# The last rotations and the bias's mask, moved ahead of the value turns and the last key chunk

## The reference

```python
h = modulate(x, sh1, sc1)
u = h @ w_in_l
q_a = apply_axial_rope(split_heads(u[..., OFF_AQ:OFF_AK], A_Q_HEADS), *rope)
k_a = apply_axial_rope(split_heads(u[..., OFF_AK:OFF_AV], A_KV_HEADS), *rope)
v_a = split_heads(u[..., OFF_AV:OFF_BQ], A_KV_HEADS)
q_b, k_b, v_b = ...                     # slices of u too, 4 heads each
o_a = window_gqa_latent(q_a, k_a, v_a, kc_a, vc_a, a_sink[l])
o_b = neighbourhood_latent(q_b, k_b, v_b, kc_b, vc_b, nat_bias[l])
o_c = conformer_conv(u[..., OFF_C:], conv_w[l], conv_b[l], conv_ln_g[l], conv_ln_b[l])
o = jnp.concatenate([o_a, o_b, o_c], axis=-1) @ w_out[l]
```

## Time and profile before

| | |
|---|---|
| median of 3 executions | 2954.65 us (2952.22 to 2955.24) |
| the profiled execution | 2943.12 us |
| its span, first to last instruction | 2941.3 us, 35988 instructions |
| mean granted TensorE clock | 0.961 of full speed |
| PE busy | 2727.4 us, 93% of the span |
| VectorE, ScalarE busy | 991.0 us, 622.2 us |
| DMA | 582 MB, mean 198 GB/s |
| `project2` up to its end, first layer | barrier seen by PE at 1229.4 us |
| `project2` up to its end, second layer | barrier seen by PE at 2252.3 us |

### The profile page before, as it was taken

How to read it: one execution, slowest core, us unless ns; L and a number is a source line. 1 busy time by engine, 2 the same in 40 slices (tenths; PEclk the granted TensorE clock), 3 DMA queues, 4 the chain that set the end, 5 groups by cost and what they waited for, 6 DMA issues and landing times. The chain is left out here.

```text
span 2941.3 us, 35988 instructions
## 1 busy us (share of the span) xinstructions
PE 2727.4 (93%) x15314; PEld 1573.6 (53%) x15314; DVE 991.0 (34%) x2175; ACT 622.2 (21%) x1297; POOL 63.4 (2%) x61
## 2 busy tenths in 40 slices
PE   8998879899999989899679999999798986999998
PEld 7776645588874456574333333333585743444443
DVE  3513445223330238385611111111573752111212
ACT  4222215211110111272401000000313621000102
POOL 0000000000000000000001111111000000000000
PEclk9999979999999999999889999999898998999999
DMA  4137671122222031100369999999120027999995
GB/s 156 65 116 284 231 312 37 72 72 79 79 86 88 0 141 44 43 2 29 143 248 371 385 384 387 381 390 392 52 72 29 16 104 295 404 422 422 422 422 238
DMA packets 87476, 582.00 MB, mean 198 GB/s; under 512 B 10186, under 2 KB 11754, under 8 KB 21780
## 3 DMA queue, kind: packets, MB, share of 16 engines
q1 hardware_dynamic: 78244, 554.66, 47.9%
q0 software_dynamic: 6544, 21.24, 2.5%
q10 hardware_dynamic: 2528, 3.80, 0.3%
HBM read 561.96 MB, written 17.70 MB: 197 GB/s over the span
## 5 line engine op out<-in xcount | busy, mean ns | idle before, releaser
L1998 PE MATMUL ps<-both,ring 128*128 128x257 f32 x1408 | 308.6, 381 | 1.6 <-PEq L1628 1.6
L2911 PE MATMUL ps<-ring,xsL 128*64 128x512 f32 x1320 | 297.5, 602 | 5.7 <-ACTq L217 5.7
L1998 PEld LDWEIGHTS ps<-both,ring 128*128 128x128 f32 x1408 | 268.2, 191 | 42.0 <-issue 1.9
L2911 PEld LDWEIGHTS ps<-ring,xsL 128*64 128x64 f32 x1320 | 100.7, 139 | 193.7 <-issue 187.7
L3142 DVE TENSOR_TENSOR hidL<-hidL,ps 128x1024 f32<-128x1024 f32 x16 | 19.5, 1222 | 463.7 <-PE ps L2911 463.7
L1816 PE MATMUL ps<-ring,actT 128*128 128x512 f32 x352 | 153.6, 598 | 6.9 <-PEq L1986 6.9
L2510 PE MATMUL ps<-both,ring 128*128 128x384 f32 x480 | 157.5, 490 | 1.9 <-PEq L1809 1.9
L2911 PE MATMUL ps<-ring,htL 128*64 128x512 f32 x640 | 145.2, 605 | 3.4 <-ACTq L217 3.2
L856 PE MATMUL ps<-both,ring 128*128 128x264 f32 x640 | 143.8, 386 | 1.5 <-PEq L633 1.5
L3172 ACT ACTIVATE hidL<-ps 128x1024 f32<-128x1024 f32 x16 | 16.4, 1024 | 555.2 <-PE ps L2919 318.5
L856 PEld LDWEIGHTS ps<-both,ring 128*128 128x128 f32 x640 | 121.4, 190 | 23.0 <-issue 2.4
(11 more groups left out here) (536 smaller groups left out, 3671.6 us busy)
## 6 DMA issues: line engine op xcount, KB each, us to landing
ring<-in_w_exp SPq DMA_DIRECT2D x245, 1024.0 KB, 12.9
ring<-in_w SPq DMA_DIRECT2D x73, 1024.0 KB, 5.1
tokens_b<-in_w_exp SPq DMA_DIRECT2D x63, 1024.0 KB, 12.4
ring<-in_w_mod SPq DMA_DIRECT2D x48, 1024.0 KB, 5.2
h<-in_w_exp SPq DMA_DIRECT2D x37, 1024.0 KB, 17.1
lent<-in_w_exp SPq DMA_DIRECT2D x26, 1024.0 KB, 15.5
both<-in_w_exp SPq DMA_DIRECT2D x13, 1024.0 KB, 18.1
gb<-in_rows SPq DMA_DIRECT2D x8, 512.0 KB
```

The source lines that it names most:

```text
L1998: mm = pe.matmul(k.ps[:, 4 * (j % 2) + 2 * gv + h, 0:HALF], w(c_), hT[:, c_, FIRST + h * HALF:FIRST + (h + 1) * HALF], start=c_ == 0, stop ...
L2911: mm = pe.matmul(ps[HD * par:HD * par + HD, bank + half, :], lhsL(kk, par), weights(kk)[:, half, par, :], start=kk == 0, stop=kk == KD - 1 ...
```

## The change

The change alters the order of statements only; no instruction is added or removed. On PE, `rotate(3)` moves from behind job 19 to behind `turn_back`, which follows job 17. `rotate(4)` moves from behind job 20, the last one, to behind job 18. `turn_values` stays behind job 19. On VectorE the mask's six passes move ahead of the three copies to `vb`.

```diff
                 elif i == VB:
                     turn_back()
+                    rotate(3)
+                elif i == VB + 1:
+                    rotate(4)
                 elif i == KB:
-                    rotate(3)
                     turn_values()
-                elif i == KB + 1:
-                    rotate(4)
...
             for r in range(2, 5):
                 rope(r)
-            dve.wait_ge(turned.sem, turned.of(1))
-            for t in range(0, NT2, 2):
-                at = 4 * BANK + t * 2 * P
-                steps.free(dve.tensor_copy(vb[:, t:t + 2, :], psf[:, at:at + 4 * P].rearrange("p (t c) -> p t c", t=2)))
             dve.wait_ge(z_done.sem, z_done.of(1))
             to, mt = 0, 0
             for _, lo, hi in NEAR_PIECES:
...
                 steps.free(dve.tensor_tensor(out, mask, src, ALU.subtract))
                 to, mt = to + GRID_H * w, mt + w
+            dve.wait_ge(turned.sem, turned.of(1))
+            for t in range(0, NT2, 2):
+                at = 4 * BANK + t * 2 * P
+                steps.free(dve.tensor_copy(vb[:, t:t + 2, :], psf[:, at:at + 4 * P].rearrange("p (t c) -> p t c", t=2)))
             steps.join()
```

## The result

The changed kernel took 2935.44 us (median of 4, 2932.73 to 2936.02) against 2954.94 us for the kernel before: a ratio of 0.9943, 95% interval 0.9929 to 0.9957, so 12.7 to 21 us less. (The two medians are 19.5 us apart, which would be a ratio of 0.9934; the ratio of 0.9943 stands for 16.8 us.) The prediction was 13.5 us less. Over all timed executions of the two, 15 of the changed kernel average 2936.2 us and 59 of the one before 2951.4, a difference of 15 us. The four of the kernel before in the first comparison average 2954.4 us: its 19.5 us caught that kernel at the upper end of its scatter.

What follows compares the result with a forecast made beforehand. The prediction took PE's wait for VectorE at the barrier ending `project2` as the bound. 11.8 us from that wait plus 1.7 from the clock made 13.5 less: 2954.65 to 2941.1 us, 8-in-10 range 2935 to 2946.5.

Steps and rivals of the forecast that it cites:

- What bounds: Barrier ending `project2`: VectorE alone, late behind PE's last rotation, makes PE wait 7.57 us per layer.
- The rotations and the mask: In `project2`: moved rotations add no PE wait; mask and copies run beside jobs 18 to 20, at no cost.
- The wait that is left: Barrier ending `project2`: ScalarE becomes last, PE idles about 1.65 us; 5.9 us less per layer, 11.8 in all.
- Passed on: Behind attention: the experts' weight stream moves forward with PE, costed at nothing; rival of gain not passed on, chance 0.07.
- My sign of being wrong: Wrong if the second layer's experts end less than 9 us earlier; other signs were a long wait or late SP or ScalarE.
- The clock: Start of attention: first score group at full clock, then a fall; 0.87 us per layer, 1.7 in all, bounds 0 to 6.3.
- holds in one layer: Rival, chance 0.27 for one or both layers: clock stays full in attention; one layer gives about 2.2 us more.
- a later fall lands worse: Part of the rival of no clock gain or a little loss elsewhere, chance 0.15: 9 to 12 us less in all.
- my reading of it on the barrier's idle time alone: Attention: idleness cut from 7.57 to about 1.65 us would leave 2.4 GHz in both layers, the upper case, 18 us.
- The sum: Whole kernel: 11.8 us from the barrier wait plus 1.7 from the clock, 13.5 us less, 2941.1 us.
- the range: Whole kernel's time, 8 in 10: 2935 to 2946.5 us.

Runs made afterwards that it cites:

- a late VectorE: Changed kernel with the mask's six passes done eight times over on VectorE; ratio 1.0010 to the kernel before.
- The filled runs: Constant matmuls added: 16 or 8 behind the last rotation of the kernel before (1.0051, 0.9996), or in the changed kernel's gaps (0.9944; with split copies 0.9949).
- the two with filled gaps: Changed kernel with constant matmuls behind job 20 and the first two score groups, ratio 0.9944 to before; the same with the last key product's copies split, 0.9949.
- the one with both edits: Changed kernel with constant matmuls in PE's gaps and the last key product copied by ScalarE and VectorE; ratio 0.9949 to before, median 2936.1 us.

## Why the prediction was right

**What bounds.** Right: the last rotation, issued last, made VectorE late, and no other engine was. Rotation 4 alone gives the full gain, rotation 3 and the mask none, and a late VectorE takes it all back.

**The rotations and the mask.** Costed at nothing, no wait added: right. The rotations wait for nobody; the mask ended at 1211.29, 18.8 us behind the start of `turn_back`, where I had computed 18.7. The cover of the copies is the last job, about 10 us: they end 9.63 us before ScalarE does; my times gave 1223.04 - 1213.4 = 9.6.

**The wait that is left.** Forecast 5.9 us per layer, measured 6.03 by the wait and 6.01 and 5.90 by the stages. The barrier behind ScalarE took 0.31 us where I had put 0.45 (0.39 by the earlier trace rows), so the wait that is left, 1.54 us, is just under the 1.6 that I had called the shortest. The 5.90 us of the second layer are less than the wait's 6.03 because PE's own part of that stage took 0.12 us more.

**Passed on.** Right: the final norm starts as much earlier as the stages before it say, and the experts' DMA stream moves along with PE. The two stages that the change does not touch differ by +0.87 and +0.08 us. In the first of them PE was at half clock for about 3 us more (77.9 us against 74.7), so what I had costed at nothing took 0.95 us in this profile; in the two further ones it took 0.90 us and gave 1.3. My sign of being wrong, experts that end less than 9 us earlier, was badly put: in this profile the final norm starts only 7.4 us earlier, because the first 1046 us took 6.2 us longer; counted from the first `project2` it is 13.6.

**The clock.** This term was mis-sized, within its bounds. Forecast 0.87 us in each layer, 1.7 in all; measured 1.90 + 0.73 = 2.6. The mechanism that I took for likeliest, first group at full clock and a fall behind it, is what the second layer does. In the first layer the clock held through all of attention, so that VectorE took the first head's result 11.6 us after the start of attention instead of 14.7, and 1.3 of these 3.2 us went again in a fall in the gate rows, a place where the kernel before had none in this layer. The two further profiles of the changed kernel show the same. My "holds in one layer" and "a later fall lands worse" thus both happened, in one profile. The filled runs show that the gaps between the score groups matter: the clock fell with 0.71 and with 0.30 us of idleness at the barrier, and it held in both layers once the gaps were filled. In the second layer it fell in all five profiles with a wait of 1.54 or 1.26 us and open gaps, and held in the two with filled gaps. But in the first layer it held through the same open gaps in four of those five, and fell there in the two with less idleness at the barrier, 0.71 and 0.30 us. What decides between these is open. The rule of the Trainium skill ("TensorE: Matmul & The Clock Gate", Part 1), that activity holds the clock and its lack brings it down, agrees with the filled runs; my reading of it on the barrier's idle time alone, full clock in both layers, does not: after 1.54 us the clock fell in the second layer. Why the same open gaps did no harm in the first layer, the rule as I read it doesn't say.

**The sum.** 11.8 + 1.7 = 13.5 forecast; 11.9 + 2.6 = 14.5 in the stages; 15 on average over the executions. The first median of 19.5 us less lies at the edge of the range (2935.4 against 2935.0). I had read the scatter of the kernel before off three executions, 2952 to 2955 us; fifty-nine of them range from 2944.9 to 2956.4. In the stages that it was made of, the forecast was 1 us short, not 6. That the whole stretch to the final norm gives 13.6 us, almost the forecast, is in part luck: the clock gave 0.9 us more than I took, and the untouched stages took 0.95 us that I had left out; in one of the further profiles the same stretch gives 15.4 us.

## What to carry to other kernels

At a block's end look at what hangs on the last instruction of the busiest engine: here a matmul of 0.86 us that another engine had to follow with 7 us of passes cost TensorE 6 us per layer, and one job earlier it cost nothing. Moving it as far as just ahead of one long job was enough; the order of the passes behind it did not matter. And judge such an edit by the stages it touches: in three profiles of the changed kernel they repeat within 0.5 us, while whole executions scatter by 10. Look at the stage behind them too, because a fall of the clock can move over the cut.

## What the runs showed of the hardware

- The granted clock fell to 0.5 in the start of attention after only 0.71 us of idleness at the barrier, while PE ran groups of 1.15 us with gaps of 1.5 us. With matmuls of constants in the gaps it held in both layers, and the score groups started no later. With the gaps open and 1.54 us of idleness it also held in the first layer of four profiles and fell in the second layer of the same four; why is open.
- The same first 1046 us of the program took from 1046.1 to 1056.8 us over the profiles, at a mean granted clock of 0.97 in the shortest and 0.95 in the longest. The 10.66 us between these two are all PE's busy time, 971.45 against 982.11 us:

```profile
0.00:1046.14 1046.14, 971.45 (x5645) 696.26 (x5645) 346.83 (x712) 241.23 (x487) 0.20 (x4) 0.97 0.34 122
```

```profile
0.00:1056.80 1056.80, 982.11 (x5644) 702.12 (x5645) 347.07 (x712) 241.21 (x487) 0.20 (x4) 0.95 0.34 121
```

  The first row is of the kernel before, the second of the one with both edits. One place where such a difference arises: between 255 and 280 us the kernel before was granted the full clock throughout, the changed kernel 0.86 on the mean, in the same part of the program, and PE got through 259 matmul records there instead of 304:

```profile
255.00:280.00 25.00, 21.85 (x304) 17.68 (x300) 11.35 (x26) 9.52 (x22) 0.00 (x0) 1.00 0.64 216
```

```profile
255.00:280.00 25.00, 21.85 (x259) 16.11 (x255) 10.93 (x25) 9.69 (x22) 0.00 (x0) 0.86 0.47 169
```

  Again the first row is of the kernel before, the second of the changed one. Why the clock fell there in one execution and not in the other is open.
- A barrier that ended behind ScalarE let PE go 0.31 us later, one that ended behind VectorE 0.53 to 0.54. In another block it was 0.39 us behind ScalarE, so the first figure is that of this barrier.
